# The depthwise convolution of a hybrid decoder step: history sums of the sample rows, convolution state laid out by channel, order of VectorE and shares of the taps

## What is computed

```python
def conv_module(h, state, w_pw1, b_pw1, w_dw, b_dw, ln_g, ln_b, w_pw2, b_pw2):
    u = h @ w_pw1 + b_pw1
    a, gate = jnp.split(u, 2, axis=-1)
    u = a * jax.nn.sigmoid(gate)
    full = jnp.concatenate([state.astype(u.dtype), u], axis=1)
    c = lax.conv_general_dilated(full, w_dw[:, None, :].astype(u.dtype), window_strides=(1,),
                                 padding='VALID', dimension_numbers=('NWC', 'WIO', 'NWC'),
                                 feature_group_count=D_MODEL) + b_dw
    c = jax.nn.silu(layer_norm(c, ln_g, ln_b))
    y = c @ w_pw2 + b_pw2
    new_state = full[:, -(CONV_WIDTH - 1):]
    return y, new_state
```

## Time and profile before

| | us |
|---|---|
| median of 3 runs | 2221.11 (2218.87 to 2223.14) |
| the profiled execution, its own time | 2221.3 |
| its span, first to last instruction | 2219.6 |
| PE busy in it | 2132.1 (96%) |
| DVE busy | 1027.1 (46%) |
| ACT busy | 732.8 (33%) |
| POOL busy | 273.3 (12%) |

### The profile page before, as it was taken

How to read it: one execution, slowest core, us unless ns; L and a number is a source line. 1 busy time by engine, 2 the same in 40 slices (tenths; PEclk the granted TensorE clock), 3 DMA queues, 4 the chain that set the end, 5 groups by cost and what they waited for, 6 DMA issues and landing times.

```text
span 2219.6 us, 39410 instructions
## 1 busy us (share of the span) xinstructions
PE 2132.1 (96%) x16225; PEld 2080.0 (94%) x16225; DVE 1027.1 (46%) x1266; ACT 732.8 (33%) x1132; POOL 273.3 (12%) x222
## 2 busy tenths in 40 slices
PE   8999999888789999999999999999999899999997
PEld 8999999878679999999999999999987799999997
DVE  4444433289966444433254443233455464444322
ACT  5222222376754222222232222222333242222222
POOL 0000001168823000001100000121000030000000
PEclk9999999988899999999999999999999999999999
DMA  4332233311103323322233223332224133332321
GB/s 139 91 89 85 83 88 88 97 39 57 39 24 95 95 85 88 91 82 84 82 98 92 85 85 87 88 91 77 67 58 142 58 96 95 90 90 85 95 79 67
DMA packets 338765, 185.67 MB, mean 84 GB/s; under 512 B 6012, under 2 KB 334942, under 8 KB 338668
## 3 DMA queue, kind: packets, MB, share of 16 engines
q1 hardware_dynamic: 335228, 172.78, 26.9%
q0 software_dynamic: 3200, 11.64, 1.6%
q10 hardware_dynamic: 256, 0.10, 0.0%
HBM read 177.29 MB, written 8.05 MB: 84 GB/s over the span
## 4 chain that ended last, share of the span: by engine, by line
PE 84%; DVE 10%; issue 3%; ACT 2%; DMA 1%; POOL 0%; ACTq 0%; SPq 0%; DVEq 0%
PE ps L438 76%; PE ps L459 4%; DVE ps L1464 3%; DVE w_lo L425 1%; DVE prod L1505 1%; ACT w_hi L418 1%; PE ps L1115 1%; DMA hist_in<-in_state_conv 0%; PE ps L1121 0%; DVE cv L1511 0%; PE ps L1054 0%; DMA pin<-in_gla_onorm_g 0%; PE ps L1062 0%; DVE x L1542 0%; DVE cv L1513 0%
## 5 line engine op out<-in xcount | busy, mean ns | idle before, releaser
L438 PE MATMUL ps<-xg_hi,w_hi 128*128 128x272 f32 x3344 | 696.9, 290 | 4.2 <-DVE tb L1479 2.2
L438 PE MATMUL ps<-xg_hi,w_lo 128*128 128x272 f32 x3344 | 693.6, 289 | 0.0
L438 PE MATMUL ps<-xg_lo,w_hi 128*128 128x272 f32 x3344 | 691.1, 288 | 0.0
L418 ACT ACTIVATE w_hi<-raw 128x1024 fp32r<-128x1024 f32 x329 | 347.7, 1059 | 1020.7 <-PE ps L438 970.3
L425 DVE TENSOR_TENSOR w_lo<-raw,w_hi 128x1024 fp32r<-128x1024 f32 x329 | 425.8, 1296 | 446.3 <-ACT w_hi L418 445.8
L438 PEld LDWEIGHTS ps<-xg_hi,w_hi 128*128 128x128 f32 x3344 | 528.6, 189 | 7.6 <-DVE tb L1479 2.6
L438 PEld LDWEIGHTS ps<-xg_lo,w_hi 128*128 128x128 f32 x3344 | 527.2, 189 | 0.0
L438 PEld LDWEIGHTS ps<-xg_hi,w_lo 128*128 128x128 f32 x3344 | 523.6, 189 | 0.0
L438 PE MATMUL ps<-h_hi,w_hi 128*128 128x272 f32 x1536 | 318.2, 288 | 1.7 <-DVE x L1542 0.9
L438 PE MATMUL ps<-h_hi,w_lo 128*128 128x272 f32 x1536 | 317.9, 288 | 0.0
L438 PE MATMUL ps<-h_lo,w_hi 128*128 128x272 f32 x1536 | 316.7, 288 | 0.0
(11 more groups left out here) (266 smaller groups left out, 1506.0 us busy)
## 6 DMA issues: line engine op xcount, KB each, us to landing
raw<-in_ffn_w_gate SPq DMA_DIRECT2D x88, 512.0 KB, 3.8
raw<-in_ffn_w_up SPq DMA_DIRECT2D x88, 512.0 KB, 3.8
raw<-in_ffn_w_down SPq DMA_DIRECT2D x64, 512.0 KB, 4.0
raw<-in_gla_w_in SPq DMA_DIRECT2D x25, 512.0 KB, 3.8
raw<-in_ffn_w_down SPq DMA_DIRECT2D x32, 384.0 KB, 3.3
raw<-in_conv_w_pw SPq DMA_DIRECT2D x24, 512.0 KB, 4.0
raw<-in_gla_w_out SPq DMA_DIRECT2D x8, 512.0 KB, 4.0
st<-in_state_gla POOLq DMA_DIRECT2D x4, 1024.0 KB, 9.6
```

Source lines behind the costliest of these rows:

```text
L418: nc.scalar.activation(w_hi[:, n % RING], raw[:, n % RAW], ACT.Copy).then_inc(w_high, 1)
L438: last = nc.tensor.matmul(ps[:, 2 * pair + c, 0:HALF], w[:, r, k, :], a[:, k0 + k, c * HALF:(c + 1) * HALF], start=(k0 + k == 0 and w is w ...
```

## The change

The history enters by channel: the host passes `state_conv` once more as an array of 128 partitions by 8 blocks by 8 samples by 30 rows (`state_conv_by_channel`), and POOL loads it with one DMA into `hist` early in the first FFN. DVE computes the sums over the history in the first FFN's up loop, one channel block in each of iterations 1 to 8 (`dve_history`): four products, one sum, one addition of the bias, into `hsum`. In the convolution stage a block's sample rows are then four small operations on the new rows (`dve_samples`), each of which adds a product to what the one before it left, behind a semaphore. PE's transposes of the history, ACT's copies of them, and the wait `c_tre` are gone. `u` of all 544 rows is one operation.

DVE's order in a block is new. After the gate product it does `low` of two slots (those whose `high` ACT did in the block before), then `pool_part`, then 5 of its taps (EARLY), the value product, `u`, 3 taps, `u_lo`, the remaining taps, and the sample rows. ACT does its two `high` behind the products for POOL and no longer ahead of `u_hi`. `pool_sum` has 4 buffers in place of 2. Shares of the taps: 6 PE, 12 POOL, 13 DVE in blocks 0 to 5; 7, 12, 12 in block 6; 14, 8, 9 in block 7. PE takes the mean of a block one block earlier.

The state goes out by channel: `tail`, its transposes and copies are gone, SP writes the last columns of `uext` with one DMA (`conv_tail`, behind the loads of `pw2`), POOL copies the 26 kept rows from the input as before (`conv_kept`), and the host puts the pieces together.

```diff
-        PE_TAPS = [6] * (M - 2) + [8, 16]
-        POOL_TAPS = [13] * (M - 2) + [12, 7]
+        PE_TAPS = [6] * (M - 2) + [7, 14]
+        POOL_TAPS = [12] * (M - 2) + [12, 8]
...
+        def dve_history(dve, i):
+
+            m = i - 1
+            taps_of_block = wdw[:, :].rearrange("p (j m) -> p j m", m=M)[:, 0:HIST, bass.ds(m, 1)].rearrange(
+                "p j o -> p o j")
+            for t in range(DEC):
+                n = HIST - t
+                last = nc.vector.tensor_tensor(hist_prod[:, :, t, 0:n], hist[:, m, :, t:HIST],
+                                               taps_of_block[:, :, 0:n].to_broadcast([P, NB, n]), ALU.mult)
+            last.then_inc(c_hsum, 1)
+            dve.wait_ge(c_hsum, 3 * i - 2)
+            nc.vector.tensor_reduce(hsum[:, m, :], hist_prod[:, :, :, :].rearrange("p b t j -> p (b t) j"), AX_X,
+                                    ALU.add).then_inc(c_hsum, 1)
+            dve.wait_ge(c_hsum, 3 * i - 1)
+            nc.vector.tensor_scalar(hsum[:, m, :], hsum[:, m, :], par[:, bass.ds(C_BDW + m, 1)], None,
+                                    ALU.add).then_inc(c_hsum, 1)
...
+            if s is f00:
+                with dve.Fori(0, 1) as i:
+                    up_pair(i)
+                dve.wait_ge(c_hist, 16)
+                dve.wait_ge(c_zero, 1)
+                with dve.Fori(1, M + 1) as i:
+                    up_pair(i)
+                    dve_history(dve, i)
...
             load_square(sp, pw2, conv_w_pw2[0])
+            sp.wait_ge(c_u, M)
+            sp.dma_start(conv_tail, uext[:, :, SEQ:UEXT]).then_inc(c_tail, 16)
             load_ffn(sp, f01)
...
+            nc.gpsimd.memset(hist_prod[:, :, :, :], 0.0).then_inc(c_zero, 1)
+            pool.wait_ge(u_init, M)
+            pool.dma_start(hist[:, :, :, :], state_conv_by_channel).then_inc(c_hist, 16)
...
-            for b in range(2):
-                pool.dma_start(hist_in[0:NB // 2 * HIST, b, :],
-                               state_conv[0, b * NB // 2:(b + 1) * NB // 2, :, :].rearrange("b t d -> (b t) d")
-                               ).then_inc(c_hist, 16)
...
-            pool.wait_ge(c_tte, 2)
...
+            pool.wait_ge(c_out, 16)
+            pool.wait_ge(c_tail, 16)
             pool_square_sum(pool, x, 2, lambda m: (evac, pw2.u0 + m + 1))
...
-            pe.wait_ge(c_hist, 32)
-            for m in range(M):
-                wait(pe, c_tre, 2 * (m // 4))
...
-                if m >= 3:
-                    mean(m - 3)
+                if m >= 2:
+                    mean(m - 2)
...
-                high(act, pw1.s0 + 2 * m + AHEAD)
-                high(act, pw1.s0 + 2 * m + 1 + AHEAD)
                 act.wait_ge(c_u, m + 1)
                 wait(act, c_pe, m - 1)
                 nc.scalar.activation(u_hi[:, p, 0:USPAN], uext[:, m, 0:USPAN], ACT.Copy).then_inc(c_uhi, 1)
-                wait(act, c_fin, m - 1)
+                wait(act, c_fin, m - 3)
                 for j in range(POOL_TAPS[m]):
...
+                high(act, pw1.s0 + 2 * m + AHEAD)
+                high(act, pw1.s0 + 2 * m + 1 + AHEAD)
                 if m + 1 < M:
                     diagonals(m + 1)
...
+            def dve_samples(m):
+
+                out = cv[:, m, SEQ:T].rearrange("p (b t) -> p b t", t=DEC)
+                new = uext[:, m, USPAN:UEXT].rearrange("p (b t) -> p b t", t=DEC)
+                old = hsum[:, m, :].rearrange("p (b t) -> p b t", t=DEC)
+                for d in range(DEC):
+                    wait(dve, c_samp, DEC * m + d if d else 0)
+                    nc.vector.scalar_tensor_tensor(
+                        out=out[:, :, d:DEC], in0=new[:, :, 0:DEC - d], scalar=tap(HIST - d, m),
+                        in1=(out if d else old)[:, :, d:DEC], op0=ALU.mult, op1=ALU.add).then_inc(c_samp, 1)
...
+            EARLY, MID = 5, 8
             for m in range(M):
...
                 nc.vector.tensor_tensor(halves(tb[:, p, :]), bank_pair(0), halves(rB[:, :]), ALU.mult).then_inc(evac, 1)
                 if m:
-                    dve_taps(m - 1, 4 + (m - 1) % 2)
+                    low(dve, n - 2 + AHEAD)
+                    low(dve, n - 1 + AHEAD)
+                if m >= 2:
+                    pool_part(m - 2, 4 + m % 2).then_inc(c_fin, 1)
+                if m:
+                    dve_taps(m - 1, 4 + (m - 1) % 2, 0, EARLY)
...
+                nc.vector.scalar_tensor_tensor(out=uext[:, m, HIST:UEXT], in0=ta[:, p, :],
+                                               scalar=par[:, C_BPW1 + m:C_BPW1 + m + 1], in1=tb[:, p, :],
+                                               op0=ALU.add, op1=ALU.mult).then_inc(c_u, 1)
+                if m:
+                    dve_taps(m - 1, 4 + (m - 1) % 2, EARLY, MID)
...
+                if m:
+                    dve_taps(m - 1, 4 + (m - 1) % 2, MID, TAPS)
+                dve_samples(m)
+            dve_taps(M - 1, 0, 0, TAPS)
+            low(dve, pw1.s0 + 2 * M - 2 + AHEAD)
+            low(dve, pw1.s0 + 2 * M - 1 + AHEAD)
             pool_part(M - 2, 4 + M % 2).then_inc(c_fin, 1)
```

More of the change, by code:

```diff
@@ L135, in build @@
         uext = at("uext", [P, M, UEXT], F32, A0)
[L136 to L146, removed]
+        o = A0 + M * UEXT * 4
+        pool_sum = at("pool_sum", [P, 4, SEQ], F32, o)
+        o += 4 * SEQ * 4
         wdw_hi = at("wdw_hi", [P, TAPS * M], F32R, o)
@@ L968, in _ @@
                     if g == 0:
[L969 to L970 removed]
                         taps(m - 1)
[L972 removed]
+                if m == 2:
                     pe.wait_ge(s_nv, 3 * 1 + 1)
[L974 to L975 removed]
+                if m >= 2:
+                    mean(m - 2)
             taps(M - 1)
[L977 removed]
             pe.wait_ge(evac, pw2.u0)
[L980 to L984 removed]
             mean(M - 2)
@@ L1216, in _ @@
             act.preload_act_table(ACT.Sigmoid)
-            for m in range(4):
-                act.wait_ge(c_tr, m + 1)
-                dst = uext[:, 2 * m:2 * m + 2, HIST + SEQ:UEXT].rearrange("p m (b t) -> p m b t", t=SEG)
-                for b in range(2):
-                    last = nc.scalar.activation(
-                        dst[:, b, :, 0:HIST],
-                        ps[:, 4 + m % 2, b * NB * HIST:(b + 1) * NB * HIST].rearrange(
-                            "p (b t) -> p b t", t=HIST), ACT.Copy)
-                last.then_inc(c_tre, 1)
             def diagonal(m, j):
@@ L1279, in _ @@
             act.preload_act_table_set(LN_EXP)
-            act.wait_ge(c_tt, 1)
-            act.wait_ge(c_samp, 3 * M)
-            for b in range(2):
-                nc.scalar.activation(tail_out[0:HIST + NS, b * 512:(b + 1) * 512], ps[0:HIST + NS, 2 + b, :],
-                                     ACT.Copy).then_inc(c_tte, 1)
             for m in range(M):
@@ L1446, in _, with dve_taps @@
             dve_rsqrt(dve, 1, 3, (s_stat, 2))
-            dve.wait_ge(c_zero, 1)
-            dve.wait_ge(c_tre, 4)
+            dve.wait_ge(c_zero, 2)
             dve.wait_ge(c_wdw, 1)
             nc.vector.tensor_tensor(wdw_lo[:, :], wdw[:, :], wdw_hi[:, :].bitcast(F32), ALU.subtract).then_inc(c_wdw, 1)
-            def dve_taps(m, bank):
-                for step in range(DVE_TAPS[m]):
+            def dve_taps(m, bank, first, end):
+                for step in range(first, min(end, DVE_TAPS[m])):
                     j = PE_TAPS[m] + POOL_TAPS[m] + step
@@ L1774 @@
     arrays, args = {}, {}
-    for name, value in inputs.items():
+    laid = dict(inputs)
+    history = np.asarray(inputs["state_conv"])[0]
+    laid["state_conv_by_channel"] = history.transpose(2, 0, 1).reshape(8, 128, 8, 30).transpose(1, 0, 2, 3)
+    for name, value in laid.items():
         a = np.ascontiguousarray(value)
@@ L1782 @@
     r = run_bass_kernel_spmd(nc, [arrays], core_ids=[0])
-    return tuple(r.results[0][f"out_{name}"] for name, _ in OUTS)
+    out = {name: r.results[0][f"out_{name}"] for name, _ in OUTS}
+    tail = np.asarray(out["conv_tail"]).transpose(2, 1, 0).reshape(62, 1024)
+    new_conv_prompt = np.ascontiguousarray(tail[None, None, 0:30])
+    new_conv_sample = np.concatenate([np.asarray(out["conv_kept"]), tail[30:].reshape(8, 4, 1024)], axis=1)[None]
+    return (out["y_prompt"], out["y_sample"], new_conv_prompt, out["new_gla_prompt"], new_conv_sample,
+            out["new_gla_sample"])
```

102 lines of the change are left out of this document (29 added, 73 removed).

## The result

The median after is 2202.9 us (2201.7 to 2203.6) against 2221.0 (2218.9 to 2223.1): a ratio of 0.9919, 95% interval 0.9905 to 0.9933. The change takes off 18.2 us; the forecast was 16.1, and 2205 us lay 2.1 us off. The profiled execution after has a span of 2201.2, 18.4 less than before.

A forecast was written before the change was run, and what follows sets the result against it. DVE was taken to set the pace mid-stage, with waits for the history and PSUM at the start. From 2221.3 us, -11.2 - 3.4 - 2.8 + 1.3 = -16.1 gave 2205 us, range 2197 to 2220.

The forecast's parts named there:

- The start: Convolution stage up to the first `u`: without history wait, transposes and copies, the sigmoid comes earlier; -11.2 us.
- The first block: From first to second `u`: DVE waits for ACT's `high`, yet the step takes 21.1 us against 24.5; -3.4 us.
- Six blocks: The six later steps between `u`: 22.0 us each in place of 22.5, six times giving -2.8 us.
- three blocked and one free: The four sample steps on DVE in each block, beside POOL's adds: 4.0 us, between 1.0 and 5.7.
- the floor: Lower limit on a block from DVE's wait for `high`: 21.8 us, just hidden under the forecast 22.0.
- the rival with free sample steps: In the blocks, sample steps at 1.0 us and `u_lo` free, so the wait on `high` bounds; 2198 us, chance 0.14.
- The tail: Behind the last `u`: 9.0 us removed, eight more taps (6.3) and sample steps (4.0) added; +1.3 us.
- Moved, with one answer each: History sums and DMA in the first FFN, POOL's `conv_tail` wait, PE's earlier mean: each put at 0 us.
- The wait of POOL on `conv_tail`: Ahead of POOL's squares: 0 us, 8.5 at most; squares well after 671 less the gain would count against it.
- That every step meets a whole add: Rival in blocks and tail: samples 5.7 us, `u_lo` +1.1, blocks 24.3; 2220 us, no change, chance 0.17.
- That the wait on `high` makes the kernel slower: Rival: DVE's steps slow POOL's first five adds, `high` comes late, blocks take 26.2 us; 2232 us, chance 0.08.
- That the history isn't hidden: Rival in the first FFN: eight iterations at up to 4.0 us, 2237 us; chance 0.06 shared with something else.

The follow-up runs named there:

- ring of 8: The changed kernel with 8 places in place of 6 in the ring of products between ACT and POOL; 2192.2 us, ratio 0.9863.
- `high` early: The changed kernel with ACT's two `high` moved back ahead of `u_hi`; 2191.8 us, ratio 0.9868.
- its doubling: The changed kernel with the history's products and sum done twice in each iteration of the first FFN; 2199.9 us, one execution.
- history alone: The kernel before with only the history sums moved to the first FFN and the state by channel; DVE's order and tap shares unchanged; 2184.9 us, ratio 0.9837.
- order of before with new shares: The history moved and the state by channel, with the new tap shares but the order and place of `high` of before; 2186.5 us, ratio 0.9846.
- new order with shares of before: The changed kernel with the tap shares of before, DVE one tap fewer; 2206.2 us, ratio 0.9934.
- seven taps on PE: Against the kernel with only the history and state moved, one tap per block goes from POOL to PE in blocks 0 to 5; 2182.3 us, ratio 0.9824.
- the run with added products: The changed kernel with eight unused products on PE right before the means of blocks 6 and 7; 2201.1 us, ratio 0.9903.

## Why the prediction was right, and where its steps were not

**The start** was forecast at -11.2 and is -11.05 (up to 1.3 more in the other kernels with the same start); ACT's chain to the sigmoid is the one that I laid out. **The first block**, -3.4, is -3.74: DVE sits idle for 6.86 us until `high`, as the chain of five adds, a product and a `high` said. Its `low` then starts at 447.33, 10.9 us after the first `u`; the forecast was 11.0.

**Six blocks**, forecast at -0.5 each, are -0.80 each, -4.8 in place of -2.8, and here two terms were mis-sized and hid each other. The sample steps were put at 4.0 us, "three blocked and one free". They cost 2.1. By shape, in eight blocks (xcount | busy us, mean ns | idle):

```profile
L1459 DVE SCALAR_TENSOR_TENSOR cv<-uext,wdw,cv 128x16 f32<-128x16 f32 x8 | 8.4, 1051 | 0.3
...
L1459 DVE SCALAR_TENSOR_TENSOR cv<-uext,wdw,hsum 128x32 f32<-128x32 f32 x8 | 3.6, 447 | 0.0
L1459 DVE SCALAR_TENSOR_TENSOR cv<-uext,wdw,cv 128x8 f32<-128x8 f32 x8 | 2.8, 351 | 0.3
L1459 DVE SCALAR_TENSOR_TENSOR cv<-uext,wdw,cv 128x24 f32<-128x24 f32 x8 | 2.0, 244 | 0.3
```

One of the four is blocked: the third (16 columns) in seven blocks, at 1.17, and the last one in block 0. The first costs 0.37 in the middle blocks and is blocked too in block 7, at 1.10. What decides is where in POOL's adds a step starts:

```profile
486.94 0.24 DVE L1459 SCALAR_TENSOR_TENSOR cv<-uext,wdw,cv 128x24 f32<-128x24 f32 x1
486.99 1.36 POOL L837 TENSOR_TENSOR pool_sum<-pool_sum,tap_prod 128x512 f32<-128x512 f32 x1
487.22 1.17 DVE L1459 SCALAR_TENSOR_TENSOR cv<-uext,wdw,cv 128x16 f32<-128x16 f32 x1
```

The add before this one ends at 486.85. The second step starts between the two adds and runs through; the third starts during the add and ends at 488.39, just behind its end (488.35). So it is for all 32 steps of the trace: the 15 that start while an add runs end 0.03 to 0.06 us behind that add, the 17 others take 0.23 to 0.25.

`u_lo`, at half of its blocked price in the forecast, is blocked whole: 1.82 where it was 0.72, +1.1 and not +0.55. With these two the block's own work is 22.52 - 5.8 + 0.79 + 2.1 + 1.1 = 20.7; the trace has 21.72 - 0.80 = 20.9. That falls below the floor that I had worked out from the wait on `high`, 21.8, so the floor became the bound: 21.72 in every block. In my text it was a floor that "stays just hidden", with DVE "hardly idle before `low` in later blocks", and the case where it binds was the rival with free sample steps (2198). What happened is that rival's mechanism at a price between the two, which is why the median lies between 2198 and 2205. Shortening the wait by 1.8 us (ring of 8) or taking it away (`high` early) shows it.

**The tail** was +1.3 and is +0.3: its sample steps are 1.10 + 1.73 = 2.8, not 4.0, and the rest of the sum holds within 0.5 us (the bias that it takes off at a mean of 0.80 took 0.24 in this block).

**After the tail** I took the work to follow as before, and that step failed: +1.9, by PE's clock. I had counted PE's mean and the state's transposes as 0, since they ran ahead of DVE's last addition. As time on the path they are 0. But with them and two taps gone from the end of PE's work in the stage, and DVE's tail no shorter, PE stands idle for 5.16 us, and the means and the first variances behind that run at 0.50 of its clock.

**Moved, with one answer each.** The history in the FFN is hidden: 3.9 us under a cover of 11. Its DMA cost nothing (6.1 us to land). The wait of POOL on `conv_tail` I bounded by the landing time, 8.5 us, and that bound was wrong, though the cost of nothing was right. POOL's squares begin at 664.62, where 670.76 less the gain is 653: 11 us late, and the forecast named this as a sign against it. The term left out is the issue: SP gets to this DMA at 657.46, behind the loads of `pw2`, and it lands 7.0 us later.

```profile
664.62 1.09 POOL L543 TENSOR_TENSOR acc<-x 128x544 f32<-128x544 f32 x1 [48.34 <-DMA out_conv_tail<-uext]
...
687.75 1.72 POOL L550 TENSOR_TENSOR acc<-acc,sqt 128x544 f32<-128x544 f32 x1
```

POOL's last sum of them starts at 687.75; before it was 705.36, 17.6 earlier with all of the lateness made up.

**The rivals.** That every step meets a whole add (2220), with the Trainium skill's rule ("SBUF — State Buffer", section "Who interferes with whom"), fails at "every", not at the rule. The trace agrees that a step which meets a running add waits for its end: `u_lo` starts at 480.97, 0.07 us into an add, and takes 1.82 in place of 0.72; the third sample step takes 1.17 in place of 0.24. But POOL's next add isn't always under way when a step is done: some 0.14 us lie between two adds (486.85 to 486.99), and a short step that starts in them passes. That the wait on `high` makes the kernel slower didn't come: POOL's adds stayed at 17.69/11 = 1.61 us, far from the 2.05 at which it would decide (a block of 24.9 there by its own terms, not 24.7). The wait does bound the block, but at 21.72. That the history isn't hidden is refuted by its doubling.

Summed by DVE's trace, -11.05 - 3.74 - 4.84 + 0.32 = -19.3, and +1.9 behind it, so -17.4, against -16.1. The span fell by 18.4; where the last 1.0 us came behind the norm no run shows. The time was forecast within 2.1 us partly by luck: the sample steps priced too high (the blocks and the tail gave 3.0 more than forecast) and the clock that was left out (1.9 less) stand against each other. What the forecast didn't see is that the same removal without the new order is worth 36. I priced the order's gains and waits together with the history's, as one sum per block, and never worked out the block of before's order without the history.

## What to carry to other kernels

When a change removes work and reorders what is left, work out the removal alone as well: here it gave twice what both gave together. A rounding or a copy put behind a producer that is throttled by a small ring inherits the consumer's pace, and two more places in the ring, or a place ahead of it, gave back 11 us. Work that is off the path may still hold up TensorE's clock for the step that is on it, so look at how long PE will be idle ahead of a short product before calling its removal free.

## What the hardware showed that I had not expected

Whether a short VectorE step with its inputs in SBUF is blocked beside POOL's adds is decided by its start alone. Of the sample steps in five of the kernels here (after, history alone, order of before with new shares, new order with shares of before, seven taps on PE) all 59 that start during an add are held to its end, and all 101 others run at 0.23 to 0.25 us. With dependent steps one behind another the blocking often alternates: a step held to the end of an add lets the next start between two adds and pass, and the one after it meets the next add (1.16, 0.25, 1.16 and 0.24 us with the shares of before). So a chain of such steps isn't priced by a chance for each: place its start against the adds and follow it through.

The granted clock of PE stood at 0.50 for products behind 5.16 us of idle PE, and at 1.00 for the same products behind 2.05 us (new order, shares of before). In the run with added products 1.93 us of idle time were followed by slow products too (3.57 us for eight), and there the clock was at 1.00 at the end of the idle time and at 0.50 two microseconds later, so idle time by itself doesn't tell the level.
